# Three norms without a shift: rows rounded as they come, inverse roots multiplied in behind the products

## What is computed

```python
def rms_norm(x, gain):
    y = x * lax.rsqrt(jnp.mean(x * x, axis=-1, keepdims=True) + EPS)
    return y * gain
# first block, last lines
x = x + g2 * conv_ffn(ada_norm(x, norm2_g, sh2, sc2), p)      # up1, down1
x = rmsnorm(x, final_norm_g)                                  # "normf"
# second block
h = concat([meta, x])                                         # 16 + 512 tokens
h = h + fox_mixer(rms_norm(h, attn_norm), ...)                # "norm3", fox projection
h = h + swiglu(rms_norm(h, ffn_norm), w_in, w_out)            # "norm4", up2, down2
return rms_norm(h, final_norm)[:, 16:]                        # "norm5"
# fox_mixer: q, k, v, gate, f_logit = split(h @ w_in); q and k get a norm per head,
# log_f = log_sigmoid(f_logit + b_f), attention with decays, times sigmoid(gate), @ w_out
# swiglu: (silu(gate) * up) @ w_out
```

## Time and profile before

| | us |
|---|---|
| median of 3 runs | 1827.69 (1826.71 to 1830.38) |
| the profiled execution | 1831.44 |
| its span, first to last instruction | 1829.4 |
| TensorE matmuls busy | 1722.5 (94%) |
| TensorE weight loads busy | 1390.0 (76%) |
| VectorE busy | 869.7 (48%) |
| ScalarE busy | 619.2 (34%) |
| GpSimd busy | 95.3 (5%) |
| mean granted TensorE clock | 0.955 of 2.4 GHz |
| median landing of the e16, e2, e4 loads behind down1 | 2.5 |

### The profile page before, as it was taken

How to read it: one execution, slowest core, us unless ns; L and a number is a source line. 1 busy time by engine, 2 the same in 40 slices (tenths; PEclk the granted TensorE clock), 3 DMA queues, 4 the chain that set the end, 5 groups by cost and what they waited for, 6 DMA issues and landing times.

```text
span 1829.4 us, 20326 instructions
## 1 busy us (share of the span) xinstructions
PE 1722.5 (94%) x8105; PEld 1390.0 (76%) x8105; DVE 869.7 (48%) x1195; ACT 619.2 (34%) x811; POOL 95.3 (5%) x134
## 2 busy tenths in 40 slices
PE   8899978999998899999997899999998899999997
PEld 3478766888886688888786678987886788888886
DVE  4754676566664544444334432323664533333233
ACT  2342358222222333333222433243552332222221
POOL 0100000100000000000001000002331000000000
PEclk9899979999998899999998799998999899999998
DMA  9331010644453233332333121122111233332331
GB/s 325 96 106 61 26 41 30 217 159 151 140 184 110 55 94 101 101 94 64 95 95 98 46 80 59 49 92 72 37 36 47 56 106 92 92 92 85 89 102 48
DMA packets 213925, 170.28 MB, mean 93 GB/s; under 512 B 5445, under 2 KB 202949, under 8 KB 213831
## 3 DMA queue, kind: packets, MB, share of 16 engines
q1 hardware_dynamic: 207222, 144.80, 26.5%
q0 software_dynamic: 6608, 24.19, 3.9%
HBM read 166.84 MB, written 2.13 MB: 92 GB/s over the span
## 4 chain that ended last, share of the span: by engine, by line
PE 85%; DVE 9%; ACT 4%; issue 1%; DMA 0%; DVEq 0%; SPq 0%; ACTq 0%
PE PS L430 22%; PE PS L431 22%; PE PS L432 22%; PE PS L1937 2%; PE PS L439 1%; DVE WL L91 1%; DVE T L91 1%; PE PS L554 1%; ACT WH L87 1%; DVE X L102 1%; DVE SQ L102 1%; PE PS L458 1%; PE PS L448 1%; PE PS L1922 1%; PE PS L466 1%
## 5 line engine op out<-in xcount | busy, mean ns | idle before, releaser
L430 PE MATMUL PS<-XH,WH 128*128 128x512 f32 (+1 forms) x1280 | 493.2, 385 | 4.8 <-DVE WL L91 3.1
L431 PE MATMUL PS<-XL,WH 128*128 128x512 f32 (+1 forms) x1280 | 493.7, 386 | 0.0
L432 PE MATMUL PS<-XH,WL 128*128 128x512 f32 (+1 forms) x1280 | 491.5, 384 | 0.0
L91 DVE TENSOR_TENSOR WL<-WS,WH 128x2048 fp32r<-128x2048 f32 (+1 forms) x129 | 272.4, 2111 | 267.1 <-ACT WH L87 266.3
L430 PEld LDWEIGHTS PS<-XH,WH 128*128 128x128 f32 x1280 | 242.7, 190 | 59.3 <-DVE WL L91 3.0
L432 PEld LDWEIGHTS PS<-XH,WL 128*128 128x128 f32 x1280 | 242.5, 189 | 49.2
L431 PEld LDWEIGHTS PS<-XL,WH 128*128 128x128 f32 x1280 | 242.3, 189 | 49.5
L87 ACT ACTIVATE WH<-WS 128x2048 fp32r<-128x2048 f32 (+1 forms) x129 | 228.6, 1772 | 78.1 <-PE PS L432 61.5
L430 PE MATMUL PS<-HH,WH 128*128 128x512 f32 x352 | 137.2, 390 | 2.2 <-DVE WL L91 2.0
L432 PE MATMUL PS<-HH,WL 128*128 128x512 f32 x352 | 137.0, 389 | 0.0
L431 PE MATMUL PS<-HL,WH 128*128 128x512 f32 x352 | 136.9, 389 | 0.0
(11 more groups left out here) (331 smaller groups left out, 2388.3 us busy)
## 6 DMA issues: line engine op xcount, KB each, us to landing
WS<-in_w_in SPq DMA_DIRECT2D x24, 1024.0 KB, 5.2
WS<-in_ffn_w_up SPq DMA_DIRECT2D x44, 512.0 KB, 5.0
WS<-in_ffn_w_in SPq DMA_DIRECT2D x44, 512.0 KB, 4.8
MSRC<-in_w_mod POOLq DMA_DIRECT2D x32, 512.0 KB, 4.7
WS<-in_fox_w_in SPq DMA_DIRECT2D x16, 1024.0 KB, 5.6
WS<-in_ffn_w_down SPq DMA_DIRECT2D x16, 704.0 KB, 4.6
WS<-in_ffn_w_out SPq DMA_DIRECT2D x16, 704.0 KB, 4.6
MODW<-in_w_mod SPq DMA_DIRECT2D x8, 1024.0 KB, 11.0
```

The costliest lines, as they stand in the source:

```text
L91: self.e.tensor_tensor(o, a, b, op).then_inc(*self.done.to(*key))
L430: e.matmul(o, lh, rh, start=first and i == 0, stop=False)
L431: e.matmul(o, lh, rl, start=False, stop=False)
L432: ins = e.matmul(o, ll, rh, start=False, stop=last and i == n - 1)
```

## The change

All norms concerned have no shift, so the inverse root is one factor per token, a column of every product of the normed rows. The change uses that in three places.

- normf and norm3, now one: in down1, behind each new X[k], VectorE multiplies by both gains (G12 = final_g x attn_g), ScalarE rounds, VectorE subtracts (`gained_act`, `gained_dve`). ScalarE squares X twice, plain and with the first gain, and VectorE keeps two sums (T[2], RST). `between_*` is gone. `roots_*` makes both inverse roots: eight one-column matmuls behind q0 and q1, two roots and reciprocals, eight diagonals, spreads inside and behind q3. ScalarE copies the product of both into RST (528 columns, ones for the meta tokens), and TensorE turns it into columns behind q4 for the v rows.
- The fox projection: q, k, gate and the forget row leave PSUM by a multiply with RST on VectorE, v by a scale on ScalarE; the squares are taken from the copies. q0 to q7 lie in banks 3, 4, 0, 1, 2, 0, 1, 2; the heads matmuls of q0 to q6 move behind q4 (0, 1), q5 (2, 3), q6 (4, 5) and q7 (6). The first inverse root is multiplied into X behind q4 to q7, two row tiles each.
- norm4: the same gained rows in out2; sums behind the first two products of up2, the spread behind the next two. up2's VectorE multiplies both products out of PSUM by RST, ScalarE takes the silu in place. Both up layers use six banks instead of three.

```diff
+    URING = (1, 2, 0, 4, 5, 6)
 def up_pe(e, s, j0, norm, c0, conv):
             if f == 0:
+                if conv:
+                    e.wait_ge(*dve.at(norm, "scaled", 0))
+                prod_by_rows(e, [up_bank(0), up_bank(1)], tm, lambda k: dve.at(norm, "lo", k), (s, 1))
+                if not conv:
+                    e.wait_ge(*dve.at(norm, "sum", 7))
+                    sums_pe(e, norm, T[2], L, True, True, (norm, "sums"), step=1)
...
+                prod(e, up_bank(n), tm[m], (s, n))
+                if n == 3 and not conv:
+                    spread_pe(e, norm, L)
 def up_act(a, s, j0, norm, conv):
+            if f == 0 and not conv:
+                hi_chunk(a, j0 + 1)
+                root_act(a, norm, L, step=1)
+                hi_chunk(a, j0 + 2)
+                e.wait_ge(*pe.at(norm, "spread"))
+                a.act(RST[:, 0:L], bank(3), ACT.Copy, key=(norm, "inverse"))
+            elif f != 1 or conv:
+                hi_chunk(a, j0 + f + 1)
...
-                a.act(f1, b0, ACT.Silu, key=(s, "first", f))
+                e.wait_ge(*dve.at(s, "first", f))
+                a.act(f1, f1, ACT.Silu, key=(s, "silu", f))
 def up_dve(v, s, j0, norm, conv):
-                e.wait_ge(*acts.at(s, "first", f))
-                v.tt(f1, f1, b1, ALU.mult, key=(s, "second", f))
+                e.wait_ge(*pe.at(s, 2 * f + 1))
+                v.tt(f1, b0, RST[:, 0:L], ALU.mult, key=(s, "first", f))
+                v.tt(T[0][:, :], b1, RST[:, 0:L], ALU.mult)
+                e.wait_ge(*acts.at(s, "silu", f))
+                v.tt(f1, f1, T[0][:, :], ALU.mult, key=(s, "second", f))
...
+    def gained_act(a, name, k):
+        a.e.wait_ge(*dve.at(name, "gained", k))
+        a.act(XH[:, k, 16:NT], SQ[:, k, 16:NT], ACT.Copy, key=(name, "hi", k))
+    def gained_dve(v, name, k, gain):
+        v.ts(SQ[:, k, 16:NT], xk(k), gain, None, ALU.mult, key=(name, "gained", k))
+        v.e.wait_ge(*acts.at(name, "hi", k))
+        v.tt(XL[:, k, 16:NT], SQ[:, k, 16:NT], XH[:, k, 16:NT].bitcast(F32), ALU.subtract, key=(name, "lo", k))
+    def down1_act(a):
+        for k in range(8):
+            for h in range(2):
+                hi_chunk(a, DN1 + 2 * k + h + 1)
+            gained_act(a, "norm3", k)
+            if k >= 2:
+                a.e.wait_ge(*dve.at("norm3", "sum", k - 1))
+            a.act((T[0] if k else T[2])[:, :], xk(k), ACT.Square, key=("normf", "square", k))
+            a.act(T[1][:, :] if k else RST[:, 0:L], xk(k), ACT.Square, scale=vec("final_g", k), key=("norm3", "square", k))
+            if k == 1:
+                meta_act(a)
+    def down1_dve(v):
...
+            v.stt(xk(k), bank(DRING[k % 4]), modcol(5, k), xk(k), ALU.mult, ALU.add, key=("down1", "x", k))
+            gained_dve(v, "norm3", k, SM[:, G12 + k:G12 + k + 1])
+            if k:
+                v.e.wait_ge(*acts.at("norm3", "square", k))
+                v.tt(T[2][:, :], T[2][:, :], T[0][:, :], ALU.add, key=("normf", "sum", k))
+                v.tt(RST[:, 0:L], RST[:, 0:L], T[1][:, :], ALU.add, key=("norm3", "sum", k))
+            if k == 1:
+                meta_dve(v)
...
+    def residual_dve(v, k):
+        v.stt(xk(k), xk(k), vec("final_g", k), bank(5), ALU.mult, ALU.mult, key=("normf", "full", k))
...
+    QB = (3, 4, 0, 1, 2, 0, 1, 2)
+    Q_HEADS_AT = {4: (0, 1), 5: (2, 3), 6: (4, 5), 7: (6,)}
 def foxp_pe(e):
+                    roots_sums_pe(e)
+                elif m == 3:
+                    prod(e, bank(QB[m]), tm[:4], last=False)
+                    roots_spread_pe(e, "norm3")
+                    prod(e, bank(QB[m]), tm[4:], ("q", m), first=False)
+                    roots_spread_pe(e, "normf")
+                elif m >= 2:
+                    if m >= 5:
+                        e.wait_ge(*dve.at("q_rooted", m - 3))
+                    prod(e, bank(QB[m]), tm, ("q", m))
+                if m == 4:
+                    roots_turn_pe(e)
+                for y in Q_HEADS_AT.get(m, ()):
+                    heads_pe(e, "q", y, Q_HEADS, y == 0, False)
 def foxp_act(a):
+        hi_chunk(a, FOXP + 1)
+        roots_act(a)
+        hi_chunk(a, FOXP + 2)
+        e.wait_ge(*pe.at("norm3", "spread"))
+        e.wait_ge(*pe.at("normf", "spread"))
+        a.act(RST[:, 16:NT], bank(6), ACT.Copy)
+        a.act(RST[:, 0:16], ONE[:, 0:16], ACT.Copy, key=("inverse",))
         for i in range(4):
+            if i in (0, 2):
+                hi_chunk(a, FOXP + 3 + i // 2)
             for m in (2 * i, 2 * i + 1):
-                a.act(QT[:, m, :], bank((1 + m) % 3), ACT.Copy, key=("q", m))
-                heads_act(a, "q", m, bank((1 + m) % 3), L)
+                heads_act(a, "q", m, QT[:, m, :], L)
 def foxp_dve(v):
+        lo_chunk(v, FOXP + 1)
+        roots_dve(v)
+        lo_chunk(v, FOXP + 2)
+        e.wait_ge(*acts.at("inverse"))
         for i in range(4):
+            if i in (0, 2):
+                lo_chunk(v, FOXP + 3 + i // 2)
             for m in (2 * i, 2 * i + 1):
+                v.tt(QT[:, m, :], bank(QB[m]), RST[:, 16:NT], ALU.mult, key=("q_rooted", m))
                 heads_dve(v, "q", m, L)
...
+                if m >= 4:
+                    residual_dve(v, 2 * m - 8)
+                    residual_dve(v, 2 * m - 7)
...
+                v.tt(KT[:, m, :], full_key(m), RST[:, :], ALU.mult, key=("k_rooted", m))
...
+        v.tt(FB[:, :], PS[0:16, 512 * 4 + HALF0:512 * 4 + HALF0 + NT], RST[0:16, :], ALU.mult)
+        v.ts(FB[:, :], FB[:, :], vec("fox_b", 0, 0, 16), None, ALU.add, key=("forget",))
...
+                v.tt(FG[m][:, :], bank(m % 4), RST[:, 16:NT], ALU.mult, key=("fg", m))
```

More of the change, by code:

```diff
@@ L1515, in down_pe, with down_act @@
                 pe.name("w", j)
-    def down_act(a, s, j0, norm, between=None):
+    def down_act(a, s, j0, norm):
         for k in range(8):
@@ L1522, in down_act, with down_dve @@
             square_act(a, norm, k, xk(k))
-            if between and k == 1:
-                between(a)
-    def down_dve(v, s, j0, norm, part=None, between=None):
+    def down_dve(v, s, j0, norm):
         for k in range(8):
@@ L1576, in between_dve, with roots_sums_pe @@
[L1576 to L1583, removed]
+    def roots_sums_pe(e):
+        e.wait_ge(*dve.at("norm3", "sum", 7))
+        for c, tile in ((0, T[2]), (4, RST)):
+            for i in range(4):
+                ins = e.matmul(bank(5, 1, off=c + i), tile[:, 128 * i:128 * i + 128], ONE[:, 0:1], start=True, stop=True)
+        ins.then_inc(*pe.to("roots", "sums"))
@@ new lines, in roots_act, with roots_dve @@
+    def roots_act(a):
+        a.e.wait_ge(*pe.at("roots", "sums"))
+        a.act(ST[:, 0:4], bank(5, 4), ACT.Sqrt, bias=SM[:, EPSC:EPSC + 1], scale=1.0 / D, key=("normf", "root"))
+        a.e.wait_ge(*dve.at("roots", "square"))
+        a.act(ST[:, 4:8], ST[:, 4:8], ACT.Sqrt, bias=SM[:, EPSC:EPSC + 1], scale=1.0 / D, key=("norm3", "root"))
+    def roots_dve(v):
+        v.e.wait_ge(*acts.at("normf", "root"))
+        v.rcp(ST[:, 0:4], ST[:, 0:4])
+        v.tt(ST[:, 4:8], bank(5, 4, off=4), ST[:, 0:4], ALU.mult)
+        v.tt(ST[:, 4:8], ST[:, 4:8], ST[:, 0:4], ALU.mult, key=("roots", "square"))
+        v.e.wait_ge(*acts.at("norm3", "root"))
+        v.rcp(ST[:, 4:8], ST[:, 4:8])
+        v.tt(ST[:, 4:8], ST[:, 4:8], ST[:, 0:4], ALU.mult)
+        for c, tile, what in ((4, T[0], "norm3"), (0, RST, "normf")):
+            for i in range(4):
+                v.ts(tile[:, 128 * i:128 * i + 128], ID[:, :], ST[:, c + i:c + i + 1], None, ALU.mult,
+                     key=(what, "diagonal"))
@@ new lines, in roots_spread_pe, with roots_turn_pe @@
+    def roots_spread_pe(e, what):
+        b, tile = (6, T[0]) if what == "norm3" else (5, RST)
+        e.wait_ge(*dve.at(what, "diagonal"))
+        for i in range(4):
+            ins = e.matmul(bank(b, 128, off=128 * i), ONE[:, :], tile[:, 128 * i:128 * i + 128], start=True, stop=True)
+        ins.then_inc(*pe.to(what, "spread"))
+    def roots_turn_pe(e):
+        e.wait_ge(*acts.at("inverse"))
+        for c in range(5):
+            w = min(128, NT - 128 * c)
+            ins = e.matmul(bank(6, 1, p1=w, off=c), RST[0:1, 128 * c:128 * c + w], ONE[0:1, 0:1], start=True, stop=True)
+        ins.then_inc(*pe.to("inverse_turned"))
@@ L2109, in out2_pe @@
             pe.name("w", j)
-        mean_pe(e, "norm4", L)
     def out2_act(a):
@@ L2115, in out2_act @@
             for n in (2 * i, 2 * i + 1):
-                a.e.wait_ge(*dve.at("out2", n))
+                gained_act(a, "norm4", n)
                 square_act(a, "norm4", n, xk(n))
-        root_act(a, "norm4", L)
-        for k in range(8):
-            normed_act(a, "norm4", k, SQ[:, k, 16:NT], XH[:, k, 16:NT])
     def out2_dve(v):
@@ L2165, in vector @@
         out2_dve(v)
-        up_dve(v, "up2", UP2, False)
+        up_dve(v, "up2", UP2, "norm4", False)
         down_dve(v, "down2", DN2, "norm5")
@@ L2183, in scalar @@
         out2_act(a)
-        up_act(a, "up2", UP2, False)
```

(1 more changed line is left out.)

127 lines of the change are left out of this document (56 added, 71 removed).

## The result

The changed kernel takes 1810.66 us (median of 4 runs, 1807.99 to 1812.27), the kernel before 1827.2 us beside it: a ratio of 0.991 (95% interval 0.989 to 0.993), 16.5 us less. A second timing gave 1812.2 against 1827.23, ratio 0.991 (0.990 to 0.993). The forecast was 1806.7 us with a range of 1799 to 1816: the sign and the range hold, and the gain is 4.5 to 6 us smaller than the 21 forecast; the narrower range of the forecast alone, 1802 to 1811, holds the first timing and not the second. The profiled execution is 1809.7 us, its span 1807.8, its mean clock 0.963 (before 0.955).

A forecast was written before the change was run, and what follows sets the result against it. TensorE was taken to bound the kernel (85% of the chain), so only its idle or slow-clock time could be won. -18 + 4 + 1.7 - 8.4, taken as -21, gave 1806.7 us, range 1802 to 1811, with rivals 1799 to 1816.

The forecast's parts named there:

- The q stage: Down1's end to heads 7: rows product starts without the pause, four waits before heads come back; gain 18 us.
- rival 2: Freed time returns as waits: each of eight m takes 1 us more, q stage 6 to 7 later; 1816, chance 0.20.
- clock terms: q products: 2 us added to q5 and 2.5 us to q7 for TensorE's lower clock.
- Rival 1: The clock hardly falls in the new waits: -27.6 us, 1800; chance 0.17.
- Rival 3: TensorE stays at 1.2 GHz from heads 0 to the end of k7: +37.8 us, 1865; chance 0.03.
- rival 4: Another transfer or engine gates the pair by rows, so nothing gets shorter: 1828; chance 0.05.
- k=1 in down1: TensorE's wait for low weights, behind the meta norm, grows from 2.00 to 4.6 us; +4.0 with the clock (2.6 to 5.9).
- k, v, gate: Waits for QT +0.5, forget row +0.4, wait before the fox stage +0.75; together +1.7 us (0.5 to 3).
- Norm4: Out2 to up2: pair by rows ends 11.5 us earlier, 2.1 and about 1 us given back; -8.4 us.
- about 1 us, once: Start of up2: TensorE waits this long for late weights, with no second wait.
- The sum: -18 + 4 + 1.7 - 8.4 = -20.7, taken as -21 us off the 1827.7 median, giving 1806.7 us.

The follow-up runs named there:

- chunks_late: Changed kernel with the weights of the last q chunk and first k chunk issued later, behind the passes of m=1 and m=5: 1801.45 us, ratio 0.984.
- second profile of before: The kernel before, unchanged, timed and profiled once more: median 1826.04 us, ratio 1.000 against the shared runs of the kernel before, span 1825.4.
- meta_late: Changed kernel with the meta norm queued one step later, behind the two weight chunks of down1's step k=2: 1802.07 us, ratio 0.986.
- second profile of after: The changed kernel, unchanged, timed and profiled a second time beside the kernels built from it: 1812.2 us.
- filled run: Changed kernel with 7 unused matmuls added before heads 4 and 17 before heads 5, filling two TensorE waits: 1810.22 us, ratio 0.989.

## Why the prediction was right, and where it was off

**The q stage: right, to the wait.** Forecast from the handover 0: sums at 11.2 (measured 11.1), both spreads at 1.05, waits 1.4, 2.4, 1.5, 4.3 (measured 1.58, 2.21, 1.65, 4.22), heads 7 done at 74.7 (74.2), gain 18 (18.7 and 18.9 against the two profiles of before). The chain inverse, weights, four passes per m was as long as the rows of single instructions made it, so rival 2 fell. (From m=4's 54.0 to m=5's 58.8 the prediction has 0.4 us more than the 4.4 that it writes out; the trace has two small copies of the turned inverse there, 0.34 us, and heads 5 at 58.7.) Its clock terms, 2 and 2.5 us, stand for what chunks_late measured as 4.4. Rival 1 fell with it: the clock was 0.76 and 0.81 in the two stretches. Rival 3 fell, since the clock was back at 1.00 from 1054 to 1065 us, and rival 4, since the pair by rows waited for nothing.

**k=1 in down1: right.** Wait 4.66 for 4.6, 3.4 us at 0.50 behind it, +4.2 for +4.0.

**k, v, gate: +1.7 forecast, +2.3 measured.** That is the second profile of before (177.3) against after's two and meta_late's (179.6), which have equally much half-clock time in this stretch; TensorE's idle time grew from 7.9 to 10.2 us. QT's waits grew from 0.84 to 1.00 us each and from 1.93 to 2.15, as forecast; the wait before the scores by 0.8 (0.75 forecast); the gate's chunk waits 0.38 (0.4 forecast). The other 0.4 had no term: the wait for CK, the decays' tile, grew from 0.61 to 1.03.

**Norm4: -8.4 forecast, -7.8 or -6.2 measured.** This is the step that was mis-sized, by its second half. The pair by rows runs behind out2 without a pause and its sums start 11.1 us behind it. But the wait for the fourth chunk, "about 1 us, once", is 1.75, and the clock behind it was taken to stay up. In the first profile of after it does; in the second it doesn't, and up2 is 1.6 us longer. Busy of TensorE in the 6.8 us that begin with the matmul behind this wait, in the first profile:
```profile
1461.76:1468.56 6.80, 6.80 (x29) 1.00 0.56 157
```
and in the second:
```profile
1462.31:1469.11 6.80, 6.80 (x23) 0.75 0.56 157
```
The same matmuls take longer at 0.75. Of the seven profiles with this wait four have 1.00 here and the shorter up2, three have 0.75 and the longer.

**The sum.** By the stretches, second profile of after against the second of before: +4.2 - 18.9 + 2.3 + 1.3 - 6.2 = -17.3; first against first: +4.2 - 18.7 + 0.8 + 0.0 - 7.8 = -21.5. The medians give 15.0 to 16.5. So 0.6 to 2.2 us of the miss are norm4's, 0.6 are those of k, v, gate (second profiles), and up to 1.3 lie in the scores stage, where the forecast had no term: it wanders between 178.0 and 179.9 in all kernels. The change isn't needed for that: the kernel before has 179.9 in its first profile, with the same idle time as after (7.2 us) and the same mean clock of 0.95. What is left of the miss, some 1 to 2 us, is about the difference between two medians of the changed kernel (1810.66 and 1812.2). Taking the sum off the median was sound: the 4 us by which before's first profile was long lay outside the two stretches that carry the sum.

**The clock.** It falls at some waits of TensorE only, and not by their length. The 2.00 us of the earlier trace rows left it at 1.00 in both profiles of before. In the changed kernel 2.21, 4.22 and 4.66 us were followed by 5.2, 4.1 and 3.4 us at 0.50 (at the first two it fell before the wait was over), 1.75 in some profiles by a dip, and in the k stage the first two waits of 1.00 us by a dip too, the third by none:
```profile
1027.90:1033.10 5.20, 5.20 (x12) 0.50 0.00 0
...
1083.90:1087.30 3.40, 3.38 (x14) 0.56 0.21 73
...
1094.20:1097.60 3.40, 3.38 (x14) 0.55 0.00 0
...
1104.50:1108.00 3.50, 3.49 (x26) 1.00 0.26 90
```
The Trainium skill's page "TensorE: Matmul & The Clock Gate", section "A second HAM failure mode: psum-queue depth-cycling", has short idles between groups of matmuls, there in a bf16 kernel, swing the clock between its two levels. The filled run agrees: 0.60 became 1.00 when the idle went. What decides whether a given wait lowers the clock stays open. Taken as a verdict on the change, the rule misleads: the swing costs about 4.4 us in a q stage that became 18.7 shorter.

## What to carry to other kernels

A norm's scale that commutes with the next product can be multiplied in behind it, and the product then starts as soon as its rows are rounded; the gain is the pause, and what comes back is found by listing what stands on each queue between the late scale and the next weights. Look there first: here moving the weight copies, the meta norm and the residual multiplies on two queues, with nothing computed differently, gave 25 us on top of the 16 that the algebra gave. What such a move is worth depends on what else stands in the chain (0.6 us alone, 3.4 behind another one), so try them together too. And cut the span at fixed instructions: two profiles of the kernel before differ by 4 us, but in the q stretch by 0.2 and in up2 by 0.1.

## What the runs showed of the hardware

- The same wait of 1.75 us, at the same place, left the clock alone in four profiles and lowered it in three; up2 is 248.7 us long in the former and 250.3 in the latter, with nothing between. And 1.00 us in the k stage lowers the clock at some of its places where 2.00 us in down1 does not.
- Executions with the same code in a stretch differ there by how many such dips they have. In k, v, gate, at the same 10.15 us of idle time, two, three and four dips beside the waits for QT made 178.1, 179.6 and 181.0 us.
- Time that TensorE gains ahead of a wait set by VectorE is lost in it: 2.90 us in one execution of before, 4.29 in the other, with the same end.
- A gain multiply of 128x512 from SBUF with one scalar took 0.49 us on VectorE (estimated at 0.5), a tensor_tensor of that size 0.69:
```profile
991.79 0.49 DVE L96 TENSOR_SCALAR SQ<-X,SM 128x512 f32<-128x512 f32 x1
```
